# Latent attention by pairs of heads: values stationary in two 64-column halves, row sums from ScalarE, their inverses laid along tokens through memory

## What is computed

```python
CHUNK = 128; MLA_HEADS = 6; MLA_NOPE = 64; MLA_ROPE = 32; MLA_V = 64

def causal_block_attention(q, k, v, scale):      # q, k: 96 wide, v: 64 wide, 6 heads
    def one_block(args):                          # 4 blocks of 128 queries
        s = einsum('bhqd,bkhd->bhqk', q_blk, k) * scale
        s = where(k_pos[None, :] <= q_pos[:, None], s, -inf)
        p = softmax(s, axis=-1)
        return einsum('bhqk,bkhd->bqhd', p, v)

def second_block(x, ...):
    for l in range(2):
        h = rmsnorm_2(x, norm_mix_g[l])
        uv, z, xbc, dt_raw, c_q, c_kv, k_rope = split_cols(h @ w_in[l])
        y_a = gmlp_mixer(...)
        y_b = ssd_mixer(...)
        y_c = mla_mixer(...)                      # ends in causal_block_attention
        x = x + concatenate([y_a, y_b, y_c]) @ w_out[l]
        x = x + squared_relu_mlp(rmsnorm_2(x, norm_mlp_g[l]), mlp_w1[l], mlp_w2[l])
```

## Time and profile before

| | us |
|---|---|
| median of the runs | 3397.97 |
| lowest and highest of the runs | 3396.83, 3397.97 |
| span of the profiled execution | 3394.2 |
| attention of the first layer, from the first logits to the output projection's first matmul | 36.4 |

### The profile page before, as it was taken

One profiled execution on the slowest core, in us unless ns is written; L12 is line 12 of the kernel. 1 busy time (PEld: TensorE's weight loads), 2 busy tenths in 40 slices (PEclk: granted clock), 3 DMA queues, 4 the chain that ended last, 5 costly groups with the idle time before them and its releaser, 6 DMA issues.

```text
span 3394.2 us, 43403 instructions
## 1 busy us (share of the span) xinstructions
PE 3374.7 (99%) x15434; PEld 2735.0 (81%) x15434; DVE 1648.0 (49%) x1994; ACT 1052.8 (31%) x1414; POOL 1543.7 (45%) x1160
## 2 busy tenths in 40 slices
PE   9999999999999999999999999999999999999999
PEld 7888877788888888887678888887888888788887
DVE  5442236654423644223575442378580727857171
ACT  3222234332222322223433222236422123632122
POOL 4444443354444545443335444453354443335443
PEclk9999999999999999999999999999999999999999
DMA  4332322233333333333223333342233323223332
GB/s 152 98 99 93 112 76 68 75 99 99 97 101 92 100 96 96 99 106 81 69 75 96 96 99 99 93 103 55 66 96 99 96 97 75 61 70 108 95 99 81
DMA packets 496158, 311.26 MB, mean 92 GB/s; under 512 B 41792, under 2 KB 454827, under 8 KB 496043
## 3 DMA queue, kind: packets, MB, share of 16 engines
q1 hardware_dynamic: 494316, 307.21, 31.0%
q10 hardware_dynamic: 1727, 2.45, 0.2%
HBM read 305.94 MB, written 3.67 MB: 91 GB/s over the span
## 4 chain that ended last, share of the span: by engine, by line
PE 94%; DVE 4%; DVEq 1%; issue 1%; ACT 0%; ACTq 0%
PE bank L546 17%; PE bank L550 16%; PE bank L552 14%; PE bank L527 13%; PE bank L532 12%; PE bank L531 12%; PE bank L553 2%; PE mb L609 1%; DVE sd_p L2304 1%; PE bank L1155 1%; PE mb L1182 1%; PE mb L757 1%; DVEq L2089 1%; PE mb L861 0%; PE mb L901 0%
## 5 line engine op out<-in xcount | busy, mean ns | idle before, releaser
L502 POOL TENSOR_TENSOR wl<-raw,wh 128x512 fp32r<-128x512 f32 x1152 | 1542.6, 1361 | 1816.6 <-ACT wh L1332 1816.2
L1332 ACT ACTIVATE wh<-raw 128x1024 fp32r<-128x1024 f32 x576 | 608.6, 1057 | 1635.5 <-PE bank L527 840.8
L546 PE MATMUL bank<-xh,wh 128*128 128x512 f32 x2384 | 933.1, 391 | 0.0
L550 PE MATMUL bank<-xl,wh 128*128 128x512 f32 x2384 | 927.6, 389 | 0.0
L552 PE MATMUL bank<-xh,wl 128*128 128x512 f32 x2086 | 811.9, 389 | 0.0
L546 PEld LDWEIGHTS bank<-xh,wh 128*128 128x128 f32 x2384 | 447.4, 188 | 104.9 <-issue 11.8
L550 PEld LDWEIGHTS bank<-xl,wh 128*128 128x128 f32 x2384 | 447.6, 188 | 92.0 <-issue 0.5
L527 PE MATMUL bank<-hh,wh 128*128 128x512 f32 (+1 forms) x1216 | 472.5, 389 | 0.0
L532 PE MATMUL bank<-hh,wl 128*128 128x512 f32 (+1 forms) x1216 | 472.2, 388 | 0.0
L531 PE MATMUL bank<-hl,wh 128*128 128x512 f32 (+1 forms) x1216 | 472.2, 388 | 0.0
L552 PEld LDWEIGHTS bank<-xh,wl 128*128 128x128 f32 x2086 | 391.6, 188 | 82.1
(11 more groups left out here) (420 smaller groups left out, 3169.2 us busy)
## 6 DMA issues: line engine op xcount, KB each, us to landing
raw<-in_ffn_wi_dram SPq DMA_DIRECT2D x176, 512.0 KB, 3.7
raw<-in_mlp_w_dram SPq DMA_DIRECT2D x128, 512.0 KB, 3.7
raw<-in_w_in_dram SPq DMA_DIRECT2D x102, 512.0 KB, 3.6
raw<-in_ffn_wo_dram SPq DMA_DIRECT2D x88, 512.0 KB, 3.6
raw<-in_w_out_dram SPq DMA_DIRECT2D x32, 512.0 KB, 3.8
raw<-in_w_ple_gate_dram SPq DMA_DIRECT2D x16, 512.0 KB, 3.8
raw<-in_w_a_dram SPq DMA_DIRECT2D x8, 512.0 KB, 3.3
raw<-in_w_b_dram SPq DMA_DIRECT2D x8, 512.0 KB, 3.4
```

Source lines behind the costliest of these rows:

```text
L502: last = gp.tensor_tensor(wl[j][:, part], raw[j % RAW_SLOTS][:, part], wh[j][:, part].bitcast(F32), ALU.subtract)
L546: first = pe.matmul(out[0:width, :], h[:, c:c + width], rh[:, k, :], start=k == 0, stop=False)
L550: pe.matmul(out[0:width, :], h[:, c:c + width], rl[:, k, :], start=False, stop=False)
L1332: act.activation(wh[n % SPLIT_SLOTS][:], raw[n % RAW_SLOTS][:], ACT.Copy).then_inc(s.hi_ready, 1)
```

## The change

Blocks are taken by pairs of heads: 12 steps of (pair i, chunk n) take the place of 24 blocks. In each step:

- PE makes both heads' logits into two banks of a four-bank tensor `ring`, then both masks; `logits(c + 2)` waits for both exponentials of step c, so it runs two steps ahead. The transposes go to bank 0 of `mb` for the first head and bank 1 for the second. In `weighted` the values are stationary (128 by 64, the first head's in the array's lower 64 columns and the second's in the upper), and the turned exponentials move, 128 columns. The result has the pair's 128 features on the partitions, so `pair_turned` and the 65th column are gone. The last `weighted` stands behind u = 0 of `part` 0.
- ACT's exponential also gives the row sum (`accum_out`). ACT copies only the first head's turned block; DVE copies the second's (`bt_copied`). One reduction on DVE gives both heads' minima.
- The inverses of the sums lie with queries on the partitions and are wanted along the row. DVE inverts eight columns (`sums_inverted`), SP writes them to memory, element by element, waits for that, and reads each head's row of 512 back, spread over 64 partitions (two DMAs). DVE waits for these (`ir_landed`) in `pair_scaled`, which multiplies and splits a pair's output.
- On SP these DMAs stand between the loads of `w_out_2`: pair 0's behind load 3, pairs 1's and 2's behind load 4.
- The semaphores `y_added` and `y_done` become one, `y_steps`, and `toep_row` becomes a second count of `setup_read`; the waits stand where they stood.

```diff
-        o_tok = at_kb("o_tok", 46, [P, NT, 384])
+        inv_rows = at_kb("inv_rows", 46, [P, S])
+        o_pair = at_kb("o_pair", 48, [P, S])
...
+                    with nc.allow_non_contiguous_dma("a column of each query to rows of queries"):
+                        sp.dma_start(inverses.rearrange("s (n q) -> q (s n)", q=P),
+                                     row_inv[:, i % 2].rearrange("p s n -> p (s n)")).wait_op(s.ao_inv, need, "sem-ge")\
+                          .then_inc(s.ir_written, 16)
+                    sp.wait_ge(s.ir_written, back)
+                    for side in range(2):
+                        sp.dma_start(inv_rows[64 * side:64 * side + 64, :], inverses[side:side + 1, :].to_broadcast([64, S]))\
+                          .then_inc(s.ir_landed, 16)
+
+                for j in range(KT):
+                    load(B, L, S2_OUT + j, as3(KT, P), cols(a["w_out_2"], L, j * P, P))
+                    if j == 3:
+                        inverse_rows(0)
+                    elif j == 4:
+                        inverse_rows(1)
+                        inverse_rows(2)
...
                 def weighted(c):
...
+                    i, n = c // NT, c % NT
+                    pe.wait_ge(s.at_copied, at(L, 12, c + 1))
+                    pe.wait_ge(s.bt_copied, at(L, 12, c + 1))
...
+                    for j in range(n + 1):
+                        for side in range(2):
+                            last = pe.matmul(mb[64 * side:64 * side + 64, 2 + i % 2, n * P:(n + 1) * P],
+                                             v_tok[:, j, 2 * i + side, :], prob_t[:, c % 2, side, j * P:(j + 1) * P],
+                                             start=j == 0, stop=j == n)
...
+                    for side in range(2):
+                        act.activation(prob[:, c % 2, side, 0:w], ring[:, 2 * (c % 2) + side, 0:w], ACT.Exp, scale=-1.0,
+                                       bias=row_min[:, c % 2, side:side + 1], accum_out=row_sum[:, i % 2, side, n:n + 1])\
+                           .then_inc(s.ae_ready, 1)
...
+                def pair_scaled(i):
+                    dve.wait_ge(s.ao_ready, at(L, 3, i + 1))
+                    dve.wait_ge(s.ir_landed, at(L, 3 * 32, 32 * i + 32))
+                    dve.tensor_tensor(o_pair[:], mb[:, 2 + i % 2, :], inv_rows[:], ALU.mult)
...
+                for c in range(steps):
+                    if c + 2 < steps:
+                        biggest(c + 2)
+                    if c == 1:
                         scan_scaled()
+                    if c == 7:
                         scan_split()
+                    copied(c)
+                    if c % NT == NT - 1:
+                        sums_inverted(c // NT)
...
+                    if c in (6, 10):
+                        pair_scaled(c // 4 - 1)
+                pair_scaled(2)
```

More of the change, by code:

```diff
@@ L1167, in turned @@
[L1167 to L1183 removed]
+                    for side, copied in enumerate((s.at_copied, s.bt_copied)):
+                        pe.wait_ge(s.ae_ready, at(L, 24, 2 * c + side + 1))
+                        if c:
+                            pe.wait_ge(copied, at(L, 12, c))
+                        for j in range(n + 1):
+                            last = turn(mb[:, side, j * P:(j + 1) * P], prob[:, c % 2, side, j * P:(j + 1) * P])
+                        last.then_inc(s.at_ready, 1)
@@ new lines, in weighted @@
+                def weighted(c):
+                    i, n = c // NT, c % NT
+                    pe.wait_ge(s.at_copied, at(L, 12, c + 1))
+                    pe.wait_ge(s.bt_copied, at(L, 12, c + 1))
+                    if n == 0 and i == 1:
+                        pe.wait_ge(s.y_inv, at(L, 1, 1))
+                    if n == 0 and i == 2:
+                        pe.wait_ge(s.ao_done, at(L, 3, 1))
+                    for j in range(n + 1):
+                        for side in range(2):
+                            last = pe.matmul(mb[64 * side:64 * side + 64, 2 + i % 2, n * P:(n + 1) * P],
+                                             v_tok[:, j, 2 * i + side, :], prob_t[:, c % 2, side, j * P:(j + 1) * P],
+                                             start=j == 0, stop=j == n)
@@ L1184, in weighted @@
                     if n == NT - 1:
                         last.then_inc(s.ao_ready, 1)
-                def pair_turned(i):
-                    pe.wait_ge(s.ao_scaled, at(L, MLA_H, 2 * i + 2))
-                    for t in range(NT):
-                        last = turn(mb[:, 3, t * P:(t + 1) * P], o_tok[:, t, i * P:(i + 1) * P])
-                    last.then_inc(s.ot_ready, 1)
-                blocks = NT * MLA_H
-                for c in range(3):
-                    logits(c)
-                for c in range(blocks):
-                    if c + 3 < blocks:
-                        logits(c + 3)
+                steps = NT * MLA_H // 2
@@ L1201, in mla @@
                         weighted(c - 1)
-                    if c in (11, 19):
-                        pair_turned(c // 8 - 1)
-                weighted(blocks - 1)
                 pe.wait_ge(s.ae_ready, at(L, 24, 24))
@@ L1225, in mla @@
                         elif u == 0:
-                            pair_turned(2)
+                            weighted(steps - 1)
             for L in range(2):
@@ L2361, in mla @@
                     last = dve.tensor_tensor(y_sq[rows, k, :], y_sq[rows, k, :], y_sq[rows, 1, :], ALU.add)
-                last.then_inc(s.y_done, 1)
+                last.then_inc(s.y_steps, 1)
                 for h in range(3, 5):
```

153 lines of the change are left out of this document (65 added, 88 removed).

## The result

| | median of the runs | profiled span | PE busy |
|---|---|---|---|
| before | 3396.9 us (3396.1 to 3398.0, 5 runs) | 3394.2 us | 3374.7 us |
| after | 3450.1 us (3447.9 to 3450.8, 5 runs) | 3446.2 us | 3379.9 us |

The changed kernel takes 1.0154 times as long, with a 95% interval of 1.0142 to 1.0165: 53.2 us more, about 27 per layer. The forecast was 3403 us in a range of 3394 to 3415; the time lies 35 us above that range.

What follows compares the result with a forecast made beforehand. PE, busy for 99% of the span, was taken as the bound. Per layer, 4.8 us saved against 7.2 us of new waits gave +2.4, +4.8 for two layers: about 3403 us from 3397.97, range 3394 to 3415.

Steps and rivals of the forecast that it cites:

- I take 2.8, the row that goes in the same direction: Write of a pair's 1,024 single inverses to memory: assumed 2.8 us to land, with 2.2 and 5.8 for the range.
- the round trip: Pair 0's inverses to memory and back: PE waits 3.1 us per layer at step 8, 0.4 of it without DMA wait.
- The rival of the slow write: Single-element write takes 5.8 us, adding 3.0 us per layer to DVE's wait: 3409 us, slower; chance 0.34.
- `scan_scaled`: Holds DVE 2.08 us ahead of its copy of step 1, delaying step 2's transposes: 1.9 us per layer lost.
- what PE saves: Attention: 4.1 us less PE work per layer (values, `pair_turned`, neighbouring logits and masks), plus 0.7 at the end: 4.8.
- short waits: PE's gaps per layer: 0.3 at `logits(0)`, 0.6 at `logits(2)`, 0.4 without DMA wait, 1.3 in later steps.
- the halves do run side by side: Value matmuls: both array halves work in parallel, 3.4 us for a pair's four steps; the serial rival had chance 0.03.
- Pair 2, nothing: Pair 2's inverses return before `part` 1 needs them, costing PE nothing; above a 6 us write, pairs 1 and 2 reach PE.

Runs made afterwards that it cites:

- the one without the trip: Changed kernel with the inverses' write to memory, its two reads and the wait for them left out: 3406.05 us (ratio 1.0026).
- the stop made on purpose: Kernel before, with 20 ScalarE copies, a drain ahead of each, put between two exponentials in each layer's attention: 3425.92 us (ratio 1.0084).
- the one with both edits: Changed kernel without the inverses' write, reads and wait, and with `scan_scaled` ahead of the first minimum: 3393.92 us (ratio 0.9990).
- the repair: Changed kernel; PE turns inverses, written as 8 rows of 512 bytes ahead of load 3; `scan_scaled` first, `scan_split` behind step 7's copy: 3393.63 us (ratio 0.9990).

## Why the prediction was wrong, and where it was right

*The step that failed: "I take 2.8, the row that goes in the same direction".* It was the term of the write. The bounds were 2.2 and 5.8 us; measured were 8.9 to 10.6, and the round trip cost 44.1 us where the sum had 5.4 (2.7 per layer: the 3.1 less the 0.4 that would be there anyway). All three rows that bounded it were rows of other forms: the two piecewise ones were loads, whose pieces come from places far apart in memory and go to different partitions, and the one store wrote long rows. None had neighbours of 4 bytes written side by side, and that is the price. I did say that no row showed it; then the range should not have ended at a write of 7 us, just beyond the rows. The rival of the slow write had the direction and the path to PE, at 0.34; its price, 3409, came from the same rows. Two smaller steps failed with it: `scan_scaled` was undersized, and the clock stood at nothing.

*The chain of it, in layer 1, from T0 = 2378.7, the end of the unit before.* Load 3 left at T0 + 20.3 (forecast 17.0), because PE was already late; the write at 20.9 (17.6); both reads had left by 32.6 (22.1); the inverses were there at 35.0 (24.3). Of the 10.7 us, 3.3 are the late start, 7.2 the write, its wait and the issue of the reads (11.7 instead of 4.5), 0.2 the reads themselves. DVE's wait was 9.72 instead of 2.7, and PE's stop at step 8, forecast at 3.1, was 9.92. That it would stand there, behind load 3 in the queue, and that the split, a minimum and `scan_split` would come between the wait and the copy, was right line by line.

*The slow-write rival's sum, with the measured 10 us:* 3409 to 5.8 us, 0.4 more to 6, and four times 6 beyond, 3433. (Its figures for 7 and 9 us, 3414 and 3426, lie 1 us below that rule.) The runs show what is missing to 3450. *`scan_scaled`* was forecast at 1.9 us per layer, 3.8 in all, and cost 12.1, 8.3 more: 3.97 us of stop each, since the operation took 4.09 us beside POOL rather than 2.08, which makes up the difference to the forecast stop, and 2.1 us each of slower work ((12.1 - 7.9) / 2). *The clock* was in no term: I took each stop at its length. By the rival's rule the round trip is 17.9 us per layer (2.7 + 3.2 + 12), 36 in all; it cost 44.1, 8.3 more. Its stops are only 33.3 (the stops of the changed kernel less those of the one without the trip, 45.3 - 12.0), so by the medians 10.8 us are slower work behind six stops, 1.8 each. The windows above give 13.9 us of slower work for the changed kernel and 5.0 for the one without the trip, so 8.9 for the six, 1.5 each; the stop made on purpose gave 2.6. With 8.3 and 8.3, the sum stands at 3450; what PE saves (1.4 less than forecast) and the median of the kernel before (3396.9 over five runs, 1.1 below the 3398.0 that the forecast started from) all but cancel. (A run's time lies 1.8 us above its own span, not 4.) Not every stop is followed by the lower clock: the one of 2.34 us at 3037.99 in layer 2 has 1.00 in the 12 us behind it.

*What PE saves.* Forecast: -4.8 us per layer of work and +2.6 of short waits without the write and the scan (0.3 + 0.6 + 0.4 + 1.3), so -2.2. Measured, with both taken away: -3.0 in all by the medians, -1.5 per layer, in an interval of 0.3 to 6.8 us that holds the forecast's 4.4. The windows above are sharper: 55.80 us against 58.07, so -2.27 in layer 1 from the first logits on, and -2.28 in layer 2. The first logits start 0.58 us after the matmul ahead of them where they started 0.17 after it (forecast 0.3 more, within the 2.6), which leaves -1.9 against -2.2. The short waits were nearly right: 0.24, 0.33, 0.61, 0.43 and 0.42 us, 2.0 in all. The value matmuls were cheaper than I made them: 0.37, 0.79, 0.80 and 1.02 us to the next start for a pair's four steps, 3.0 instead of 3.4, so the halves do run side by side. The stretch from the first logits to the first output matmul is 33.3 us instead of 36.4 (of which PE stood for 0.9 by my own pieces, not the 0.7 of the forecast); the last `weighted` (1.0) now comes behind it, and the last `pair_turned` (0.35) is gone. Some of the spread lies outside the change: each layer has a stop of 2.46 us at the matmuls of the squares, 12 us ahead of the attention, in the kernel before too, and in layer 1 the 3.8 us from 2366.2 have a clock of 0.55 in the run without the trip and 1.00 in the one with both edits.

*"Pair 2, nothing"* held up to a write of 6 us, as the text said (with pieces of 8 bytes, landing within 6.5 us, neither place has a stop); at 10 us the last `weighted` stood 3.25 us and `part` 1 stood 3.26.

*The page cited there* (DMA: Bandwidth & Descriptors, Specifications, in the Trainium skill) says that below 512 B the DMA reads, modifies and writes. It pointed the right way, to this rival. But the runs don't bear it out as the measure of the loss: pieces of 4 bytes are all below 512 B, and took 2.4 or 10.0 us by their distance. What the page says in Rules for kernel authors, that a strided last dimension makes one descriptor per element and is better made contiguous, is what the repair follows, for 0.11 us of PE and 0.2 of DVE per pair, each to the next start.

## What to carry to other kernels

When a change needs a transfer whose form no row of the profile shows, its upper bound is not the nearest row; measure it, or keep the path of the bottleneck engine free of it. Don't write a column across partitions into adjacent words of memory; turn it first, if the matrix engine can do that beside its work. And price a stop of TensorE above its length, here by some 2 us each, and an operation on VectorE that takes two tiles from SBUF at up to double its time where GpSimd works on SBUF tiles beside it.

## What the runs showed of the hardware that I had not expected

- 1,024 elements of 4 bytes written to memory land in 10.0 us side by side, 4.4 us with 8 bytes from start to start, 2.4 us with 64; 512 side by side still take 8.5; 128 pieces of 32 bytes 1.4.
- The DMA engines are through with all 1,024 elements 1.6 us after the issue, side by side or 64 bytes apart; after that they stand idle for 7.9 us or 0.8 until the write is reported as landed.
- Three `scalar_tensor_tensor` of 128 by 512 on VectorE take 4.09 us beside GpSimd's `tensor_tensor` and 2.08 alone; GpSimd's two take 3.17 us instead of 2.50.
- After a stop of 12 us TensorE had a granted clock of 0.50 for the next 4 us and 0.77 for the 4 after; after stops of 3 to 4 us the windows show a lowered clock too (0.79 around the one at 2390.68), after one of 2.34 us they show 1.00, and after one of 2.46 us 0.55 in one run and 1.00 in another. One stop costs about 1.5 to 2.7 us beyond its length.
- A transpose of 128 by 8 costs TensorE 0.11 us to the next start between others of its kind.
